# Two-layer fp32 block on Trainium2: attention blocks regrouped inside the forgetting and dilated head pairs

## What is computed

```python
def second_block(x, ...):
    for layer in range(2):
        h = rmsnorm(x, norm_g[layer])
        qa, ka, va, fa, za, qb, kb, vb, zb, qc, kc, vc, zc, ga, gb, gc = split(h @ w_in[layer])
        ya = forgetting_attention(qa, ka, va, log_sigmoid(fa + b_forget)) * silu(za)  # 4 heads of 64, causal
        yb = dilated_mixture_attention(rope(qb), rope(kb), vb) * silu(zb)            # 6 heads, dilations 1, 4, 16
        yc = banded_attention(rope(qc), rope(kc), vc, 127, sinks) * silu(zc)         # 6 heads, window 128
        merged = sigmoid(ga) * (ya @ w_br_a) + sigmoid(gb) * (yb @ w_br_b) + sigmoid(gc) * (yc @ w_br_c)
        x = x + merged @ w_out[layer]
    return rmsnorm(x, final_norm_g)

def forgetting_attention(q, k, v, log_f):      # per head, c = cumsum(log_f)
    s = q @ k.T / 8 + c[:, None] - c[None, :]  # causal
    return softmax(s) @ v
```

## Time and profile before

| | |
|---|---|
| median of three runs | 3416.67 us (3413.94 to 3421.68) |
| span of the profiled execution, first to last instruction | 3412.5 us |
| TensorE busy | 3254.9 us (95%) |
| VectorE, ScalarE, GpSimd busy | 1971.0 (58%), 1055.3 (31%), 1622.7 us (48%) |
| mean granted TensorE clock | 0.985 of full |
| scores, transposes, values (lines 1740, 1767, 1785) busy | 131.6, 148.7, 126.5 us |

### The profile page before, as it was taken

How to read it: one execution, slowest core, us unless ns; L and a number is a source line. 1 busy time by engine, 2 the same in 40 slices (tenths; PEclk the granted TensorE clock), 3 DMA queues, 4 the chain that set the end, 5 groups by cost and what they waited for, 6 DMA issues and landing times.

```text
span 3412.5 us, 55095 instructions
## 1 busy us (share of the span) xinstructions
PE 3254.9 (95%) x22070; PEld 2604.8 (76%) x22070; DVE 1971.0 (58%) x2678; ACT 1055.3 (31%) x1725; POOL 1622.7 (48%) x903
## 2 busy tenths in 40 slices
PE   7999789898999999999999999999999999999997
PEld 6878688687888888787877777678878877776786
DVE  7445644648877777883344554566752256444665
ACT  4212344223323333344332232320343233322301
POOL 3333334146777676657822222257478422222475
PEclk9999899999999999999999999999999999999998
DMA  3121100221111111112331211143223311111332
GB/s 137 44 91 44 56 4 4 85 83 53 53 55 41 54 55 55 50 62 99 143 107 44 56 52 47 38 163 121 99 105 106 119 45 50 43 44 50 136 124 87
DMA packets 88252, 247.68 MB, mean 73 GB/s; under 512 B 13072, under 2 KB 24048, under 8 KB 86144
## 3 DMA queue, kind: packets, MB, share of 16 engines
q1 hardware_dynamic: 69664, 189.34, 16.5%
q10 hardware_dynamic: 18400, 55.63, 5.0%
HBM read 191.28 MB, written 42.12 MB: 68 GB/s over the span
## 4 chain that ended last, share of the span: by engine, by line
PE 85%; DVE 8%; ACT 2%; issue 2%; POOL 2%; DMA 0%; DVEq 0%; POOLq 0%; SPq 0%; ACTq 0%
PE ps L943 30%; PE ps L1480 11%; PE ps L1650 9%; PE ps L1510 6%; PE ps L1934 5%; PE ps L1955 4%; PE ps L1740 3%; PE ps L1767 3%; PE ps L1785 3%; DVE sc L3811 2%; PE ps L1255 1%; PE ps L1533 1%; PE ps L1231 1%; PE ps L1618 1%; POOL unit_lo L834 1%
## 5 line engine op out<-in xcount | busy, mean ns | idle before, releaser
L688 POOL TENSOR_TENSOR wH<-wraw,pv 128x1024 fp32r<-128x1024 f32 x135 | 267.0, 1978 | 1221.5 <-PE ps L943 1097.7
L943 PE MATMUL ps<-hH,wH 128*128 128x512 f32 x1488 | 473.9, 400 | 26.3 <-DVE hL L3041 11.7
L943 PE MATMUL ps<-hL,wH 128*128 128x512 f32 x1488 | 466.6, 395 | 0.0
L943 PE MATMUL ps<-hH,wL 128*128 128x512 f32 x1488 | 465.2, 394 | 0.0
L3368 DVE TENSOR_TENSOR xT<-ps,xT 128x512 f32<-128x512 f32 x544 | 366.1, 690 | 60.9 <-PE ps L1510 54.8
L690 POOL TENSOR_TENSOR wL<-wraw,wH 128x1024 fp32r<-128x1024 f32 x135 | 353.7, 2620 | 10.6
L943 PEld LDWEIGHTS ps<-hH,wH 128*128 128x128 f32 x1488 | 274.5, 189 | 88.8 <-issue 17.9
L943 PEld LDWEIGHTS ps<-hL,wH 128*128 128x128 f32 x1488 | 277.8, 189 | 59.0 <-issue 1.7
L943 PEld LDWEIGHTS ps<-hH,wL 128*128 128x128 f32 x1488 | 277.7, 189 | 57.5 <-issue 0.3
L2689 ACT ACTIVATE sc<-sc,stat 128x256 f32<-128x256 f32 (+7 forms) x256 | 171.1, 669 | 163.1 <-DVE stat L3818 102.1
L1767 PE MATMUL ps<-cst,sc 128*128 128x128 f32 x900 | 148.7, 285 | 12.5 <-ACT pt L2709 8.4
(11 more groups left out here) (545 smaller groups left out, 7244.0 us busy)
## 6 DMA issues: line engine op xcount, KB each, us to landing
wraw<-ws SPq DMA_DIRECT2D x158, 512.0 KB, 3.5
gates<-gated SPq DMA_DIRECT2D x48, 512.0 KB, 2.7
sg<-gates SPq DMA_DIRECT2D x16, 1536.0 KB, 6.5
upA<-ws SPq DMA_DIRECT2D x42, 256.0 KB, 3.3
upB<-ws SPq DMA_DIRECT2D x42, 256.0 KB, 2.6
gateA<-ws SPq DMA_DIRECT2D x40, 256.0 KB, 3.5
gateB<-ws SPq DMA_DIRECT2D x40, 256.0 KB, 2.7
xT<-park ACTq DMA_DIRECT2D x2, 4096.0 KB, 12.1
```

Of the source, the lines that this page charges most:

```text
L688: pool.tensor_tensor(wH[:, j, :], wraw[:, j, :], zero, ALU.add).then_inc(w_hi, 1)
L943: mm = pe.matmul(pair(p)[:, half * HALF:(half + 1) * HALF], wp, hp[:, k, half * HALF:(half + 1) * HALF], start=(m == 0 and n == 0), stop=( ...
```

## The change

In forgetting and dilated pairs alone:

- The gate projection goes through one bank (7), first all 24 matmuls of tokens 0 to 511, then the 24 of tokens 512 to 1023, in 14 pieces of 1 to 14 matmuls between the attention steps (`gate_slot`, written `z(half, from, to)`). Half 0 is taken out before half 1 begins.
- Scores of blocks 0 and 1 stand together; all values go to bank 6, those of blocks 0 and 1, 2 and 3, 5 and 6 together; the output of blocks 0 to 3 is made before values(4).
- Transposes go in 20 pieces (`CHUNKS`) of at most four tiles, each within one bank (4 and 5 in turn, at the end also 2 and 3), and each is copied out by itself: nine by ScalarE, eleven by VectorE.
- Gate input, tanh, gate product and output are made by halves.
- The first forgetting pair projects its keys to banks 2 and 3 as the others do.

```diff
 def score_bank(br, n, j):
-    return j * (HALF if br == "C" or n < 4 else 2 * HALF)
+    if br == "C" or n < 4:
+        return j * HALF + (P if br != "C" and n == 1 else 0)
+    return j * 2 * HALF
...
+CHUNKS = ((4, ((0, 0, 0, 1), (1, 0, 0, 2))), (5, ((0, 1, 0, 1), (1, 1, 0, 2))), (4, ((2, 0, 0, 3),)), (5, ((2, 1, 0, 3),)),
+          (4, ((3, 0, 0, 4),)), (5, ((3, 1, 0, 4),)),
+          (4, ((4, 0, 0, 4),)), (5, ((4, 1, 0, 4),)), (4, ((4, 0, 4, 5), (4, 1, 4, 5))),
+          (4, ((5, 0, 0, 4),)), (5, ((5, 1, 0, 4),)), (4, ((5, 0, 4, 6), (5, 1, 4, 6))),
+          (4, ((6, 0, 0, 4),)), (5, ((6, 1, 0, 4),)), (4, ((6, 0, 4, 7),)), (5, ((6, 1, 4, 7),)),
+          (4, ((7, 0, 0, 4),)), (5, ((7, 1, 0, 4),)), (2, ((7, 0, 4, 8),)), (3, ((7, 1, 4, 8),)))
+BY_ACT = (0, 2, 4, 6, 9, 12, 14, 16, 18)
+BY_DVE = (1, 3, 5, 7, 8, 10, 11, 13, 15, 17, 19)
...
+                def chunk(c):
+
+                    number, parts = CHUNKS[c]
+                    before = bank_before(c)
+                    if before is not None:
+                        copied(copy_name(before), copy_number(before))
+                    elif number >= 4:
+                        pe.wait_ge(sem("a_vtok"), L * 6 + i + (first + 1))
+                    pe.wait_ge(sem("at_exp"), last + max(2 * n + j for n, j, _, _ in parts) + 1)
+                    o = 0
+                    for n, j, k0, k1 in parts:
+                        buf, b = score_at(n)
+                        for k in range(k0, k1):
+                            mm = pe.transpose(bank(number)[:, o:o + P], SC[buf][:, j, b + k * P:b + (k + 1) * P], ident)
+                            o += P
                     mm.then_inc(sem("at_T"), 1)
...
+                        for name in ("at_pt0", "at_pt1"):
+                            copied(name, max(copy_number(c) for c in chunks_of(n) if copy_name(c) == name))
+                        if n == 4:
+                            pe.wait_ge(sem("at_half"), since("at_half", full_pair(L, i, first) + 1))
...
+                def products(h, m0, m1):
...
+                    if h == 1 and m0 == 0:
+                        pe.wait_ge(sem("z_in"), since("z_in", number + 1))
+                    for m in range(m0, m1):
+                        k, n = divmod(m, 3)
+                        w, x = ((wH, hH), (wH, hL), (wL, hH))[n]
+                        mm = pe.matmul(bank(7), w[:, j, k * P:(k + 1) * P], x[:, k, halves(h)],
+                                       start=(m == 0), stop=(m == 3 * KT - 1))
...
-                        col_gemm(*slots[3], p=1, between={4: value_tiles, 5: first_scores, 11: lambda: period(0),
-                                                          16: lambda: period(1), 21: lambda: period(2)})
+                        pe.wait_ge(sem("at_y"), pi + 1)
+                    z = gate_slot(L, i, first, *slots[3])
+                    z(0, 0, 6)
+                    value_tiles()
+                    first_scores()
+                    scores(1)
+                    z(0, 6, 20)
+                    scores(2)
+                    chunk(0)
+                    chunk(1)
+                    z(0, 20, 24)
+                    scores(3)
+                    values(0)
+                    values(1)
+                    chunk(2)
+                    chunk(3)
+                    z(1, 0, 5)
+                    scores(4)
+                    chunk(4)
+                    chunk(5)
+                    z(1, 5, 11)
+                    scores(5)
+                    values(2)
+                    values(3)
+                    chunk(6)
+                    chunk(7)
+                    z(1, 11, 14)
+                    chunk(8)
+                    z(1, 14, 15)
+                    scores(6)
+                    values(4)
+                    chunk(9)
+                    chunk(10)
+                    z(1, 15, 18)
+                    chunk(11)
+                    z(1, 18, 19)
+                    chunk(12)
+                    z(1, 19, 20)
+                    chunk(13)
+                    z(1, 20, 22)
+                    chunk(14)
+                    chunk(15)
+                    z(1, 22, 24)
+                    scores(7)
+                    values(5)
+                    values(6)
+                    return
...
+                    block(1)
+                    copy_chunk(0)
+                    block(2)
+                    half_gate(0)
+                    copy_chunk(2)
+                    block(3)
+                    copy_chunk(4)
+                    block(4)
+                    exponentials(5, (0,))
+                    copy_chunk(6)
+                    exponentials(5, (1,))
+                    if br == "A":
+                        unmask(5)
+                    exponentials(6, (0,))
+                    copy_chunk(9)
+                    exponentials(6, (1,))
+                    copy_chunk(12)
+                    copy_chunk(14)
+                    block(7)
+                    half_gate(1)
+                    copy_chunk(16)
+                    copy_chunk(18)
...
                 maxima(0)
+                if br != "C":
+                    maxima(1)
+                    maxima(2)
+                    half_input(0)
+                    copy_chunk(1)
+                    maxima(3)
+                    copy_chunk(3)
+                    maxima(4)
+                    half_gate(0)
+                    copy_chunk(5)
+                    maxima(5)
+                    half_output(0)
+                    copy_chunk(7)
+                    copy_chunk(8)
+                    maxima(6)
+                    copy_chunk(10)
+                    copy_chunk(11)
+                    copy_chunk(13)
+                    copy_chunk(15)
+                    maxima(7)
+                    half_input(1)
+                    reciprocals()
+                    copy_chunk(17)
+                    half_gate(1)
+                    copy_chunk(19)
+                    half_output(1)
+                    return
```

More of the change, by code:

```diff
@@ L1724, in steps, with copied @@
                 pi = L * 8 + i + first
[L1725 removed]
+                last, turned = pi * 16, transposed(br, L, i, first)
+                def copied(name, n):
+                    pe.wait_ge(sem(name), copies(br, L, i, first, name) + n)
                 def scores(n):
                     c0, c1, k0 = columns(br, n)
[L1730 removed]
+                    if n and not (br != "C" and n == 1):
                         pe.wait_ge(sem("at_max"), last + 2 * n + 2)
[L1732 to L1734 removed]
                     outs = [bank(0, 4)[:, score_bank(br, n, j):] for j in range(2)]
@@ L1743, in scores, with band_transposes @@
                                 mm.then_inc(sem("at_S"), 1)
-                def transposes(n, j):
+                def band_transposes(n, j):
                     c0, c1, _ = columns(br, n)
[L1747 to L1764, removed]
+                    if j == 0 and n >= 2:
+                        copied("at_pt1" if n % 2 else "at_pt0", n // 2)
+                    out, b = bank(4 + n % 2)[:, 2 * P * j:], band_slot(n)
@@ L1789, in period, with last_chunks @@
                 def period(n):
[L1790 to L1796, removed]
+                    if n < 7:
                         scores(n + 1)
-                    transposes(n, 0)
+                    band_transposes(n, 0)
                     if n:
                         values(n - 1)
[L1801 to L1805, removed]
+                    band_transposes(n, 1)
+                return scores, chunk, band_transposes, values, period
             def pair_end(br, L, i, first):
-                _, transposes, values, _ = steps(br, L, i, first)
+                _, chunk, band_transposes, values, _ = steps(br, L, i, first)
                 def last_block():
-                    transposes(7, 0)
+                    if br != "C":
+                        chunk(16)
+                        return
+                    band_transposes(7, 0)
                     values(6)
+                def last_chunks():
+                    if br == "C":
+                        band_transposes(7, 1)
+                        return
+                    for c in (17, 18, 19):
+                        chunk(c)
                 def values_and_rows():
@@ L1825, in head_pair @@
                 last = pi * 16
-                scores, transposes, values, period = steps(br, L, i, first)
+                scores, chunk, _, values, period = steps(br, L, i, first)
                 def rows():
```

214 lines of the change are left out of this document (136 added, 78 removed).

## The result

The changed kernel takes **3396.63 us** (median of four runs, 3390.60 to 3399.54) against 3416.52 for the kernel before (four runs, 3413.94 to 3421.68): a ratio of 0.9938, with a 95% interval of 0.9924 to 0.9952. That is 19.9 us less. The forecast was 3398 us in a range of 3386 to 3410.

The account below looks back on a forecast made before the run. TensorE bounds it: a dilated pair lasts as long as TensorE's list plus its waits. Eight pairs 20.8, first forgetting pairs -0.4, clock -1.7: 18.7 us off the median of 3416.67 gives 3398 us, range 3386 to 3410.

Parts of the forecast that it names:

- The eight pairs: Dilated pairs and each layer's second forgetting pair: 2.6 us gained in each, 20.8 us in all.
- new wait: TensorE waits the new order brings in at scores(3), values(0), chunks 11, 12 and 15: about 1.75 us a dilated pair.
- old waits: TensorE waits at scores(5), block 4's second transposes and scores(6) in the kernel before: all 2.9 us a pair go.
- the runs: Fewer TensorE runs and entries into scores or values in a dilated pair: net gain 1.45 us.
- The item called least sure: Values directly behind scores, four times a pair: an entry each loses 0.4 us of 1.45; no fixed part adds 0.6.
- One sign of being wrong: Copies of chunks 10 to 15 starting later than 0.3 us behind their tiles would show the forecast wrong.
- The first forgetting pair of a layer: Scores(2) wait 2.7 to 2.9 us for VectorE's masks and maxima, eating the 2.6 gain: -0.4 us for two pairs.
- The clock behind that wait: Some 3.4 us at 1.2 GHz behind the first forgetting pair's wait; one fall charged for two pairs, -1.7 us.
- Rival 1: Waits at the eight tail chunks 1.3 us more a pair: 3411 us at worst, 3405 at half; chance 0.16.
- Rival 2: Hardly any new wait in the pairs, cheaper entries, clock stays up: 14 us more gain, 3384 us; chance 0.10.
- Rival 4: Regrouping TensorE's runs saves nothing, only waits move: 4 us gained, 3412 us; chance 0.05.
- Rival 3: Short waits amid small pieces lower the clock in all ten pairs: 3413 us, up to 3430; chance 0.07.

Follow-up runs that it names:

- split runs: Changed kernel with four joined runs of scores or values each split by one projection matmul from the neighbouring piece: 3408.04 us, ratio 0.9968 to the kernel before.
- pieces early: Changed kernel with all 24 second-half gate projection matmuls in one run behind chunk 3, none between later blocks: 3425.99 us, ratio 1.0033 to the kernel before.
- tail cover: Changed kernel with ScalarE copying chunk 9 before block 6's first exponential and four projection matmuls, not one, ahead of chunk 12: 3387.78 us, ratio 0.9916.

## Why the prediction was right

The median of 3396.63 us lies 1.4 from the forecast of 3398. The pairs of the profiled executions gave 17.4 and 18.7 us where 18.7 was foretold. The mechanism is the one foretold, but part of the nearness is luck, by terms that cancel in the first forgetting pairs, as shown below, and by a spread of 9 us between single executions.

**The eight pairs: 20.8 foretold, 20.9 measured.** The terms hold too. From start to start in the dilated pair of the changed kernel:

| new wait | foretold | measured | read from |
|---|---|---|---|
| scores(3) | 0.17 | 0.17 | 1905.59 to 1906.08, 0.49 where 0.32 is usual (1909.66 to 1909.98) |
| values(0) | 0.19 | 0.09 | scores(3) take 1.14, four blocks are worth 1.05 |
| chunk 11 | 0.45 | 0.38 | 1923.40 to 1924.01, less 0.23 |
| chunk 12 | 0.74 | 0.78 | 1924.42 to 1925.52, less 0.32 |
| chunk 15 | 0.18 | 0.29 | six tiles 0.87, worth 0.36 + 2 x 0.11 |
| sum | 1.73, taken as 1.75 | 1.71 | |

With 2.9 of old waits gone, 1.7 new and 2.63 gained, the runs give 1.4, where 1.45 was foretold. Two counts in that 1.45 are off by one: the entries into scores or values fall to 8, not 7, and the projection runs behind transposes rise to 12, not 13; by the prediction's own prices that is 1.38. The 2.9 is a start-to-start sum of mine; by the idle times that the trace lists it is 2.52 before against 1.02 after, 1.5, and the rest of the gain is then 1.1, as TensorE's listed time says. Both readings leave 1.1 to 1.4 for the runs. The item called least sure, values behind scores, came out between its bounds: scores(6) take 1.70 in front of values (1919.06 to 1920.76), seven blocks and one fixed part and no entry, and values(4) take 1.24, five blocks and the fixed 0.15. One sign of being wrong is met by its letter: chunk 10's copy starts at 1923.71, over 0.8 us behind its last tile, since VectorE ends maxima(6) only then. The prediction's layout of the lists has it so, and nothing waits for it.

**One bank costs nothing**, as foretold: behind the first of a piece, which takes 0.32, the projection matmuls are 0.23 apart (1922.85, 1923.17, 1923.40).

**The first forgetting pair of a layer** gave its own gain back, as foretold. The wait was to be 2.7 to 2.9 us and is 2.59 and 2.45. Without it the pair is as short as the others (73.46 us), which is 2.8 and 3.1 us less than before, read from its first projection matmul, and not the 2.6 that I took. So -0.4 for the two pairs was too low by about 1.3 us.

**The clock behind that wait** is the term that was sized too low. The prediction's words were "I charge one fall for the two pairs: -1.7". The clock fell in both layers, in each of the two profiles of this kernel: for 6.8 and 3.4 us in one, 3.4 and 3.4 in the other, so 3.1 to 4.3 us of loss in place of 1.7 (what the two pairs lost beyond their waits less their own gain). In the second profile the two errors cancel (2.2 us lost in the two pairs, where 2.1 was foretold), in the first they don't (3.5). From the wait of 3.31 us in the earlier trace rows I had reckoned that a little shorter one brings the clock down in one of two; over the five profiles, of four kernels, that have this wait it was seven times in ten (below).

**The rivals.** Rival 1 (new waits twice as long) is out: the waits stand where it had them but come to 1.7 us a pair, and the hand-overs it rests on took no longer than reckoned, 0.25 to 0.3 us from the last tile to a free VectorE and 0.05 to 0.13 back. Rival 2 gave the right direction for a further edit, not for this one: with more cover and the masks early the waits are nearly gone and the clock stays up in these pairs, and the kernel then takes 3378.16 us. Rival 4 is refuted by the split runs. Rival 3 put the clock down to short waits among small pieces. The traces have it otherwise: 1.00 in all eight pairs with four or five short waits, 1.00 in the version with 11.4 us of them in three pairs, and 0.50 only behind the single wait of over 2 us. The rule of the Trainium skill that stood behind it (TensorE: Matmul & The Clock Gate, psum-queue depth-cycling: short idles between groups that cycle through PSUM banks make the clock oscillate) is not borne out by any pair here.

**Changes of kind.** The Trainium skill (TensorEngine Tiling (Array Packing), Key Properties) has every change of tiling mode drain the engine. My estimate from it was 2.2 us a pair for the runs in place of 1.45, at 18 changes left; there are 20, which makes it 1.8. By it the pair would have gained 3.0 to 3.4 us. It gained 2.63, and the runs gave 1.1 to 1.4 of that. But the split runs, which add eight changes a pair for 1.5 us, come to 0.18 each, and going from scores to values costs a run's fixed part of 0.15 and no entry. So the traces agree with the page that changes cost. That they cost unequally, as the prediction had it, these runs don't show: the prices lie too close together.

## What to carry to other kernels

Independent matmuls are worth most where TensorE would wait for a copy or a maximum: with them there in small pieces this kernel gained 20 us, and with the same matmuls placed early the rest of the regrouping gained nothing. Price a regrouping from start to start, as a fixed part for each run and an entry for each change of kind, and lay the lists of the other engines beside it. Then look for the first instance of the loop, where an engine has extra work (here two masks) that the old order covered: move that work early before the regrouping, because one long wait can also take the clock down (seven times in ten here).

## What was not expected of the hardware

- A single wait of 2.07 to 2.59 us, with TensorE full on both sides, brought the 1.2 GHz level in seven cases of ten, for 3.4 us (6.8 once), from between 0.6 us before the end of the wait and 1.2 us behind it. The ten are the two first forgetting pairs in each of the five profiles, of four kernels, that have the wait. Level down: 2.59, 2.45, 2.57, 2.42 (the changed kernel, two profiles), 2.07 (runs split, layer 1), 2.58 (pieces early, layer 0) and 2.57 (tail cover, layer 0). Level kept: 2.17 (runs split, layer 0), 2.42 (pieces early, layer 1) and 2.47 (tail cover, layer 1). So the length of the wait alone doesn't decide it, and what does stays open.
- Waits of up to 1.35 us, five of them within 13 us, left the clock at 1.00.
- Scores of 384 columns take 1.58 us at the lower level and 0.85 at the upper one, projection matmuls 0.43 and 0.23: both are stretched alike, the row-tiled scores and the full-array matmuls.
